# Filter strips of a 256-token, two-block forward pass: shifted pieces moved behind the weight splits of units 5 and 7, first attention and joined units rearranged

## What is computed

```python
def conformer_conv(h, w_in, b_in, dw, dw_b, ln_g, ln_b, w_out, b_out):
    a, g = jnp.split(h @ w_in + b_in, 2, axis=-1)
    u = a * jax.nn.sigmoid(g)
    u = lax.conv_general_dilated(u, dw[:, None, :], window_strides=(1,),
        padding=((CONV_WIDTH - 1, 0),), dimension_numbers=('NWC', 'WIO', 'NWC'),
        feature_group_count=d) + dw_b          # 31 taps, each feature by itself
    u = jax.nn.silu(layer_norm(u, ln_g, ln_b))
    return u @ w_out + b_out

# first_block, layer i: modulation vectors come from one condition row
mod = cond @ ada_w[i] + ada_b[i]
h = rms_norm(x, mix_norm_g[i]) * (1.0 + sc1) + sh1
x = x + g1 * (conformer_conv(h, ...) if i == 0 else moba_attention(h, ...))
h = rms_norm(x, mlp_norm_g[i]) * (1.0 + sc2) + sh2
x = x + g2 * (jnp.square(jax.nn.relu(h @ mlp_w1[i])) @ mlp_w2[i])
```

## Time and profile before

| | before |
|---|---|
| median of 3 runs | 1223.61 us (1222.88 to 1223.83) |
| the profiled execution | 1222.33 us |
| its span, first to last instruction | 1220.5 us |
| TensorE busy | 1187.3 us (97%) |
| VectorE, ScalarE, GpSimd busy | 901.1, 585.1, 50.5 us |
| mean granted TensorE clock | 0.985 of full speed |
| DMA | 230.09 MB, 189 GB/s over the span |

### The profile page before, as it was taken

The page is one execution under the profiler, slowest core; times in us unless marked ns, Lnnn a source line. Parts: engine busy times, 40 slices in busy tenths (PEclk is TensorE's granted clock), DMA queues, the critical chain, the costliest instruction groups (busy, mean ns, idle before and its releaser), DMA issues.

```text
span 1220.5 us, 18749 instructions
## 1 busy us (share of the span) xinstructions
PE 1187.3 (97%) x7746; PEld 1031.3 (84%) x7746; DVE 901.1 (74%) x1355; ACT 585.1 (48%) x776; POOL 50.5 (4%) x69
## 2 busy tenths in 40 slices
PE   8898999999999989999999999999999999999897
PEld 6885988888988869899999888888888888998677
DVE  6778788888878675898877675776757675677666
ACT  4655757556544374764355422332212323454763
POOL 0000000000000040000000000000000000000640
PEclk9998999999989999999999999999999999999998
DMA  9798458877758614667665354333343242342000
GB/s 370 283 289 307 148 218 305 299 289 283 294 191 325 230 52 173 220 245 259 242 250 192 146 196 149 135 109 136 138 172 138 104 144 101 127 139 104 1 2 35
DMA packets 35879, 230.09 MB, mean 189 GB/s; under 512 B 4161, under 2 KB 6465, under 8 KB 9554
## 3 DMA queue, kind: packets, MB, share of 16 engines
q1 hardware_dynamic: 35794, 228.89, 51.5%
HBM read 226.08 MB, written 1.05 MB: 186 GB/s over the span
## 4 chain that ended last, share of the span: by engine, by line
PE 82%; DVE 6%; ACT 5%; DMA 3%; issue 1%; POOL 1%; SPq 1%; ACTq 0%; DVEq 0%
PE prod L1831 18%; PE prod L1832 17%; PE prod L1833 17%; PE prod L1837 11%; PE prod L1838 6%; DMA raw<-stream 3%; DVE w_lo L1046 2%; ACT w_hi L629 2%; PE prod L1798 1%; PE misc L1993 1%; PE misc L1746 1%; PE misc L2095 1%; POOL cond L1029 1%; PE prod L1848 1%; PE misc L1790 1%
## 5 line engine op out<-in xcount | busy, mean ns | idle before, releaser
L1046 DVE TENSOR_TENSOR w_lo<-raw,w_hi 128x2048 fp32r<-128x2048 f32 x131 | 300.2, 2292 | 218.9 <-ACT w_hi L629 218.8
L629 ACT ACTIVATE w_hi<-raw 128x2048 fp32r<-128x2048 f32 x131 | 250.8, 1915 | 398.7 <-PE prod L1833 276.7
L1831 PE MATMUL prod<-X_both,w_hi 128*128 128x256 f32 (+1 forms) x848 | 273.3, 322 | 4.8 <-DVE w_lo L1046 4.1
L1832 PE MATMUL prod<-X_both,w_hi 128*128 128x256 f32 (+1 forms) x848 | 269.5, 318 | 0.0
L1833 PE MATMUL prod<-X_both,w_lo 128*128 128x256 f32 (+1 forms) x848 | 269.4, 318 | 0.0
L1831 PEld LDWEIGHTS prod<-X_both,w_hi 128*128 128x128 f32 x848 | 162.1, 191 | 19.8 <-DVE w_lo L1046 5.7
L1832 PEld LDWEIGHTS prod<-X_both,w_hi 128*128 128x128 f32 x848 | 162.3, 191 | 10.8 <-issue 0.5
L1833 PEld LDWEIGHTS prod<-X_both,w_lo 128*128 128x128 f32 x848 | 162.2, 191 | 10.6
L1837 PE MATMUL prod<-X_both,w_hi 128*128 128x512 f32 x400 | 143.2, 402 | 0.5 <-DVE w_lo L1046 0.5
L1831 PE MATMUL prod<-F_both,w_hi 128*128 128x256 f32 (+1 forms) x448 | 140.8, 314 | 0.0
L1833 PE MATMUL prod<-F_both,w_lo 128*128 128x256 f32 (+1 forms) x448 | 140.4, 313 | 0.0
(11 more groups left out here) (330 smaller groups left out, 1929.1 us busy)
## 6 DMA issues: line engine op xcount, KB each, us to landing
raw<-stream SPq DMA_DIRECT2D x202, 1024.0 KB, 4.9
V<-first_chunks SPq DMA_DIRECT2D x8, 512.0 KB, 12.6
X<-x_features SPq DMA_DIRECT2D x1, 1024.0 KB, 5.7
...
V<-cond_rows SPq DMA_DIRECT2D x1, 1024.0 KB
C<-ctx_features SPq DMA_DIRECT2D x1, 1024.0 KB, 6.9
...
```

What stands on the lines that cost most here:

```text
L629: A(halves(w)[0], raw[:, n % RING, :].rearrange("p (k c) -> p k c", k=KT), ACT.Copy).then_inc(weight_hi, 1)
L1046: ins = tt(lo, raw[:, n % RING, :].rearrange("p (k c) -> p k c", k=KT), hi.bitcast(F32), ALU.subtract)
L1831: mm(out, lhs_hi, rhs_hi, start=start, stop=False)
L1832: mm(out, lhs_hi, rhs_lo, start=False, stop=False)
```

## The change

In the front (units 3 to 10): mod chunks stand before units 6, 6, 7, 7 and 8, 8, 8, 8, 9, 9, 9, 10 (so chunks 6, 7 are mod, 8 is w6, 9, 10 mod, 11 is w7, 12 to 15 mod, 16 is w8, 17 to 19 mod, 20 is w9). `SHIFT_AT` becomes chunks 7, 11, 14 and 19 (before: 7, 10, 14, 20). ScalarE makes shifted copies 0 at s = 5 (before: 4), 1 at s = 7 (before: 5), both behind that step's `split_hi`; conv_copy(0) and copies 2 stay at s = 7, behind them. `split_hi(8)` and `split_lo(8)` move from s = 8 to s = 9, behind unit 7's gate, and conv_copy(1) stands before copies 3. Diagonal blocks 2 are built at s = 7 (before: 6), blocks 3 at s = 9 before `split_lo(8)` (before: s = 8).

In the first attention two maxima and two exponentials come first, then the split (VectorE) or the transposed copy (ScalarE), then the other two.

Units 56, 57, 134, 135, 136 and those of 66 to 83 with no mod chunk before unit w+2 (67, 68, 70, 72, 73, 75, 77, 78, 80, 82, 83) become joined: 16 units.

```diff
@@ -106,7 +106,7 @@
 FIRST_UNITS = 3
 FIRST_CHUNKS = [(part, q) for q in range(4) for part in (1, 0)]
 for s in (
-    6, 7, 7, 8, 8, 8, 8, 9, 9, 9, 9, 10,
+    6, 6, 7, 7, 8, 8, 8, 8, 9, 9, 9, 10,
     14, 15, 17, 19,
     21, 23, 25, 27, 29, 31, 33, 35,
     37, 39, 41, 42,
@@ -140,7 +140,7 @@
         STREAM += two_rows
 NS = len(STREAM)
 LAST_CHUNK = {c[1]: n for n, c in enumerate(STREAM) if c[0] == "mod"}
-SHIFT_AT = [WHERE[6], WHERE[7], WHERE[8] - 1, WHERE[9]]
+SHIFT_AT = [WHERE[6] - 1, WHERE[7], WHERE[8] - 2, WHERE[9] - 1]
 BY_DMA = [(a, g) for a in (0, 1) for g in range(SHIFTS)][:6]
 BY_ACT_COPY = [(a, g) for a in range(SHIFTS) for g in range(SHIFTS) if (a, g) not in BY_DMA]
 BLOCK_2 = VEC[2, 0, 0]
@@ -169,7 +169,11 @@
 BY_ACT = {"w1", "q", "k", "v", "a_u", "b_k", "b_v", "b_q"}
 WITH_NEXT = {"conv_a"}
 UPDATES = {"conv_out": 2, "w2": 2, "wo": 2, "a_out": 4, "b_out": 2}
-JOINED = list(range(MLP0, MLP0 + 28)) + [QKV, QKV + 1, QKV + 2, QKV + 4, QKV + 5, QKV + 6] + list(range(MLP1, MLP1 + 6))
+JOINED = list(range(MLP0, MLP0 + 28)) + [QKV, QKV + 1, QKV + 2, QKV + 4, QKV + 5, QKV + 6]
+JOINED += [WO, WO + 1] + list(range(MLP1, MLP1 + 6))
+JOINED += [w for w in range(MLP1 + 6, MLP1 + 24) if MOD_BEFORE[w + 2] == 0]
+JOINED += [B_OUT, B_OUT + 1, B_OUT + 2]
+ON_X = ("w2", "wo", "b_out")
 DRAINED = []
 ACT_DONE = {}
 X_DONE = {}
@@ -692,7 +696,7 @@
                 act.wait_ge(unit_done, w + 1)
                 if UNITS[w - 2][0] == "w1" and u[0] in ("w1", "w2"):
                     act.wait_ge(f_lo, f_index(w - 2) + 1)
-                elif UNITS[w - 2][0] == "w2" and u[0] in ("w1", "w2"):
+                elif UNITS[w - 2][0] in ON_X and u[0] in ("w1", *ON_X):
                     act.wait_ge(x_updated, X_DONE[w - 2])
                 A(dst, tiles(w, 2 * T)[:, :, T:2 * T], ACT.Copy).then_inc(block_copied, 1)

@@ -750,7 +754,7 @@
                     if f >= 2:
                         act.wait_ge(f_lo, f - 1)
                     ei = e.rearrange("p (i t) -> p i t", i=2)
-                    if w not in JOINED and w - 2 in JOINED and UNITS[w - 2][0] == "w2":
+                    if w not in JOINED and w - 2 in JOINED and UNITS[w - 2][0] in ON_X:
                         act.wait_ge(x_updated, X_DONE[w - 2])
                     A(ei, ei if w in JOINED else tiles(w, T), ACT.Relu).then_inc(drained["act"], 1)
                     act.wait_ge(drained["act"], ACT_DONE[w])
@@ -827,19 +831,24 @@
                         k = p - 5
                         act.wait_ge(alibi_out, k + 1)
                         A(XH[:, k, 0:T], misc[:, k % 2, 0:T], ACT.Copy).then_inc(acts_hi, 1)
+                    def exponents(off):
+
+                        b = p % 3
+                        for t, (a, c) in enumerate(((0, P), (P, 3 * P))):
+                            i = 2 * off + t
+                            act.wait_ge(alibi_max, 4 * p + i + 1)
+                            A(S1[off][:, b, a:c], S1[off][:, b, a:c], ACT.Exp,
+                              bias=sm[:, b, i:i + 1], scale=-1.0,
+                              accum_out=sm[:, b, 4 + i:5 + i]).then_inc(alibi_exp, 1)
+
                     if p < KT:
-                        b = p % 3
-                        for off in range(2):
-                            for t, (a, c) in enumerate(((0, P), (P, 3 * P))):
-                                i = 2 * off + t
-                                act.wait_ge(alibi_max, 4 * p + i + 1)
-                                A(S1[off][:, b, a:c], S1[off][:, b, a:c], ACT.Exp,
-                                  bias=sm[:, b, i:i + 1], scale=-1.0,
-                                  accum_out=sm[:, b, 4 + i:5 + i]).then_inc(alibi_exp, 1)
+                        exponents(0)
                     if 2 <= p < KT + 2:
                         h = p - 2
                         act.wait_ge(alibi_turned, 2 * h + 1)
                         A(PT1[0][:, h % 2, :], prod[:, 1, 0:3 * P], ACT.Copy).then_inc(alibi_copied_act, 1)
+                    if p < KT:
+                        exponents(1)
                     if p == KT + 2:
                         split_hi(WO + 1)

@@ -942,9 +951,10 @@
                 if s == B_OUT + 1:
                     attention_2(0, 2)
                 if s == CONV_OUT + 1:
+                    split_hi(CONV_OUT)
+                    conv_copy(1)
                     shift_copies(3)
-                    conv_copy(1)
-                if FIRST_UNITS < s < NW and s not in AHEAD and s not in BEHIND:
+                if FIRST_UNITS < s < NW and s not in AHEAD and s not in BEHIND and s != CONV_OUT:
                     split_hi(s)
                 if s + 2 in AHEAD:
                     split_hi(s + 2)
@@ -952,14 +962,16 @@
                     nc.scalar.preload_act_table(ACT.Sqrt)
                 if s - 2 in JOINED:
                     copy_block(s - 2)
-                if s - 3 in JOINED and UNITS[s - 3][0] != "w2":
+                if s - 3 in JOINED and UNITS[s - 3][0] not in ("w2", "b_out"):
                     drain(s - 3)
                 if s >= 2 and s - 2 not in JOINED and s - 1 != A_OUT_2 and UNITS[s - 2][0] != "conv_g":
                     drain(s - 2)
-                if s in (4, 5, 7):
-                    shift_copies((s - 3) // 2)
+                if s == 5:
+                    shift_copies(0)
                 if s == 7:
+                    shift_copies(1)
                     conv_copy(0)
+                    shift_copies(2)
                 if s == COND_2_UNIT - 3:
                     act.wait_ge(cond_loaded, 32)
                     A(cond_t, cond_2, ACT.Sigmoid).then_inc(cond_sigmoid, 1)
@@ -1521,24 +1533,29 @@

                 dve.wait_ge(params_loaded, 112)
                 for p in range(a, b):
+                    def maxima(off):
+
+                        b = p % 3
+                        slope = 2.0 ** (-8.0 * (2 * p + off + 1) / HEADS)
+                        for t, (a, c) in enumerate(((0, P), (P, 3 * P))):
+                            i = 2 * off + t
+                            vec.tensor_tensor_reduce(
+                                S1[off][:, b, a:c], score_pair(p)[:, 512 * off + a:512 * off + c],
+                                alibi[:, a:c], -slope, 3.0e38, ALU.add, ALU.min,
+                                sm[:, b, i:i + 1]).then_inc(alibi_max, 1)
+
+                    if p < KT:
+                        dve.wait_ge(alibi_scored, p + 1)
+                        if p >= 3:
+                            dve.wait_ge(alibi_turned, 2 * (p - 3) + 2)
+                        maxima(0)
                     if p >= 5 and p < KT + 5:
                         k = p - 5
                         dve.wait_ge(acts_hi, SET[4] + k + 1)
                         tt(XL[:, k, 0:T], misc[:, k % 2, 0:T], XH[:, k, 0:T].bitcast(F32),
                            ALU.subtract).then_inc(acts_lo, 1)
                     if p < KT:
-                        b = p % 3
-                        dve.wait_ge(alibi_scored, p + 1)
-                        if p >= 3:
-                            dve.wait_ge(alibi_turned, 2 * (p - 3) + 2)
-                        for off in range(2):
-                            slope = 2.0 ** (-8.0 * (2 * p + off + 1) / HEADS)
-                            for t, (a, c) in enumerate(((0, P), (P, 3 * P))):
-                                i = 2 * off + t
-                                vec.tensor_tensor_reduce(
-                                    S1[off][:, b, a:c], score_pair(p)[:, 512 * off + a:512 * off + c],
-                                    alibi[:, a:c], -slope, 3.0e38, ALU.add, ALU.min,
-                                    sm[:, b, i:i + 1]).then_inc(alibi_max, 1)
+                        maxima(1)
                     if 1 <= p <= KT:
                         e = (p - 1) % 3
                         dve.wait_ge(alibi_exp, 4 * p)
@@ -1671,13 +1688,16 @@
                     attention_1(0, 2)
                 if s == B_OUT + 1:
                     attention_2(0, 2)
+                if s == CONV_OUT + 1:
+                    build_blocks(3)
+                    split_lo(CONV_OUT)
                 if s < NW:
                     while at < WHERE[s]:
                         dots(at)
                         at += 1
                     if s in BESIDE:
                         dots(BESIDE[s], (0,))
-                    if s > FIRST_UNITS and s not in AHEAD and s not in BEHIND and s != CONV_OUT + 1:
+                    if s > FIRST_UNITS and s not in AHEAD and s not in BEHIND and s not in (CONV_OUT, CONV_OUT + 1):
                         split_lo(s)
                     at += 2 if s in BESIDE else 1
                 if s - 2 in JOINED:
@@ -1688,7 +1708,7 @@
                     drain(s - 2)
                 if s + 2 in AHEAD:
                     split_lo(s + 2)
-                if s in (3, 4, 6, 8):
+                if s in (3, 4, 7):
                     build_blocks((s - 2) // 2)
                 if s in BESIDE:
                     dots(BESIDE[s], (1,))
```

## The result

The changed kernel takes 1214.74 us (median of 8 runs, 1211.29 to 1219.95), the kernel before 1222.69 in the same set (8 runs); the ratio is 0.9946, 95% interval 0.9931 to 0.9961. In a second set it took 1214.14 against 1222.64, ratio 0.9930 (0.9912 to 0.9949). I had predicted 1212.1 between 1208.5 and 1217.5, so the time lies in the range. In the first set it lies just above the narrower 1210.5 to 1214.5 of the forecast itself, in the second just inside. By the medians the gain is 7.95 and 8.50 us, by the profiled executions 7.50 (1214.83 against 1222.33), where I had 11.5.

The account below looks back on a forecast made before the run. TensorE, 97% busy, was bounded by its waits, in the front through w8's landing and the gate queued behind it. Front -8.8, half clock +0.6, attention -1.9, joined units -1.4: -11.5, so 1212.1 us, range 1208.5 to 1217.5.

Parts of the forecast that it names:

- last piece: VectorE's last convolution piece, at the front's end: at 108.8 to 109.6 instead of 117.86, a gain taken as 8.8 us.
- walk: Step-by-step timing of the front's engines and transfers under the new order, giving 8.3 to 9.0 us gained.
- signs of a wrong forecast: ScalarE idle over 4 us before w7 or w8, unit 8 gaining under 5, new late stalls, attention turn near 3.2.
- half clock: TensorE at 1.2 instead of 2.4 GHz over part of unit 8, after waiting behind conv(3): 0.6 us lost.
- rival A: Transfers bind in the front: w7 and w8 land 4 us or more late, front gains 4.5, 1216 us; chance 0.22.
- landings: Times the front's weight chunks arrive by DMA: w7 at 70.1, w8 at 87.9, w9 near 101.5 us.
- price of six pieces: DMA time in the front for six shift transfers queued among the chunks: 3.5 us, taken as 3.8.
- B: Rival: no stall lowers TensorE's clock, front gains 10, attention 2.4, joined units 1.6, giving 1209.6 us; chance 0.15.
- C: Rival: slower, 1227 us, as w8 lands much later in the front and delays conv(3); chance 0.04.
- D: Rival: another wait stands just behind each one removed, in front and attention, so 1222 to 1224 us; chance 0.04.
- Attention: First attention: a turn falls from 3.21 to 2.86 us, four save 0.35 each, plus the last exponentials; 1.9 us gained.
- Joined units: Sixteen more units, in MLPs and b_out, at 5.65 instead of 5.76 us each: 1.4 us gained together.

Follow-up runs that it names:

- e5: The kernel before with only shifted copies 0, 1 and 2 and conv_copy(0) moved behind the splits for units 5 and 7; 1221.12 us.
- e6: The kernel before with the front's edits except the moves of shifted copies 0 to 2; 1217.12 us.
- e7: The changed kernel run once more with nothing altered; 1214.14 us against 1222.64 for the kernel before.
- e1: The kernel before with only the front's edits, without the attention's reordered loops and the longer list of joined units; 1215.56 us.
- e10: The changed kernel with VectorE's split to XL in the first attention placed behind both pairs of maxima; 1216.24 us.
- e11: The changed kernel with one mod chunk moved behind w9, two dummy matmuls before conv(3), four after, unit 136 unjoined, transfers of copies 1 one chunk later; 1210.84 us.
- e4: The changed kernel with five more dummy matmuls on TensorE between conv(3) and the token columns; 1215.19 us.
- e8: The changed kernel with one mod chunk moved from before w9 to before w10, two dummy matmuls before conv(3), four after, unit 136 unjoined; 1208.49 us.
- e9: The changed kernel with one mod chunk moved from before w9 to before w10 and nothing else; 1212.53 us.
- e12: The changed kernel with one mod chunk moved behind w9, two dummy matmuls before conv(3), two after, unit 136 unjoined, transfers of copies 1 one chunk later; 1210.30 us.

## Why the prediction was right, and where not

**The time lies in the range, and the mechanism of the front was right up to the last piece.** Unit 5 followed unit 4, w8 was waited for 1.44 us, the mean came at 101.66 (walk 100.1, late start 1.2), and in this execution the last piece came 8.5 us earlier where I took 8.8. e5 and e6 show that gate and stream carry most of it. Yet three of my own signs of a wrong forecast came up. ScalarE waited 5.92 us before w7 (7.97 in e7), over the 4 that I had named; my walk itself had some 6 us there, from 62.9 and a gate to 70.1, so that sign was ill chosen; unit 7 was not held up by it in the first profile, and by 1.1 us in e7. Unit 8 gained 3.41 us, under 5: that is the half clock below. And there are new waits, small ones, before unit 84 (0.24 us) and behind unit 136 (0.49). The range was wide enough to hold rival A's 1216 as well, to which 1214.74 is nearer than to 1212.1.

**Half clock, taken as 0.6 us, was the term most mis-sized.** It cost 3.2 us up to unit 9 in the first profile: 3.9 between last piece and unit 8, less 0.7 that came back, as unit 8 took 5.94 instead of 6.66. I had gone by the one case of the trace of before (half clock from 61.4 to 64.8 behind the wait of 3.17 us, which the earlier trace rows does not list) and let it fall on part of unit 8, where TensorE has work to spare; it fell on the chain of token columns, dummies and spread, on which everything else waits. And I had written that conv(3) may lose 2 us to a low clock for nothing. That is nearly so: in e1, e7, e10 and e11, with half clock on it, the last piece came 7.9, 7.3, 7.1 and 8.2 us behind w9, without it 7.1 to 7.6 (7.1 in the changed kernel, e4, e8 and e9, 7.4 in e12, 7.6 in e6).

**The landings were good for one execution only.** I had w7 at 70.1, w8 at 87.9, w9 at 101.5. With the starts taken off, the five traces of the new front have w7 at 69.5 to 73.6, w8 at 88.4 to 92.6 and w9 at 102.3 to 108.1. The term mis-sized here is the price of six pieces, 3.8 us from one stretch: by the estimate above it is 3.8 to 4.8 in these five, and each front has two sets up to w8. A further 1.0 us on average came before w7's pieces: the chunk ahead of w7 landed at 65.7 to 68.0 where I had 65.9. The last piece is on average at 112.2 in them and at 119.3 in the three with the old front: 7.1 gained, not 8.8. So rival A holds in part: the transfers bind once the gate no longer does, in some executions. B's 1209.6 was reached only by e8 (1208.49), with a chunk less ahead of w9 and dummies besides. Nothing speaks for C and D: w8 was never 11 us late, and the time did fall.

**Attention, 1.9 taken, 1.33 to 1.34 measured.** The turn was right (2.90 against 2.86), and three turns gave 0.74, 0.31 and 0.30 us where I had four of 0.35. The 0.5 behind the last pair did not come: from its first maximum to unit 56 it is 7.60 us, before 7.59.

**Joined units, 1.4 taken, 0.9 measured.** Units 56 and 57 gave 0.2, as worked out. The second MLP gave its 1.0 by luck: I had nine units at 0.11 each; three gave 0.11, five 0.20, and units 74, 79, 83 and 84 lost 0.4 together. In b_out units 134 and 135 gave 0.2, but the sums behind unit 136 lost 0.49 (8.65 against 8.16), where I had said mostly hidden and the term came to +0.2; e8, without it, is back at 8.16. By the rule on the pitch of matmuls in the Trainium skill, "TensorE: Matmul & The Clock Gate", section "Wait — 56ns, not 53.3ns?", it would have been an estimated 0.04 us a unit; the rows gave 0.1 or 0.2, so here the trace is against it.

**The sum** went 4.0 us too far between the two profiled executions: half clock in the front 2.6, attention and joined units 1.1, last piece 0.3, the late start 1.2, and clock and pace at units 11, 12, 45, 46 and 59 2.3; against that stand 3.5 from the faster joined units 13 to 30 and the boundary at unit 43. By the medians the gain fell short by 3.5 us (7.95 against 11.5) and the time by 2.6 (1214.74 against 1212.1). That the parts that nobody had forecast nearly cancel (3.5 for, 3.5 against with the late start) is chance.
